# A kernel of three transformer-like layers: VectorE computes the low parts of the weights one chunk of products later

## The reference, cut to what matters

```python
def first_block(...):
    mem_n = rmsnorm(mem, norm_mem)
    for i in range(2):
        h = rmsnorm(x, norm_mix[i])
        mkv = mem_n @ w_mem_kv[i]
        proj = h @ w_in[i]                      # q, k, v, memory q
        y_tok = windowed_gqa(...) if i % 2 == 0 else neighbourhood_attn(...)
        y_mem = memory_attn(...)
        x = x + concatenate([y_tok, y_mem]) @ w_out[i]
        gu = rmsnorm(x, norm_ffn[i]) @ w_gate_up[i]
        x = x + (silu(gu[..., :D_FF]) * gu[..., D_FF:]) @ w_down[i]
    return rmsnorm(x, norm_final)

def second_block(x, c, ...):
    sh1, sc1, ga1, sh2, sc2, ga2 = split(silu(c) @ w_ada + b_ada)
    xn = rms_norm(h, g_mix) * (1 + sc1) + sh1
    q, k, v, qi, ki, wi, xr, yr, gate_a, gate_b = split(xn @ w_in + b_in)   # 5448 wide
    attn = dsa_attention(q, k, v, qi, ki, wi, rel_bias)    # top 64 of 256 by an index score
    rnn = rg_lru(causal_dwconv(xr), ...) * gelu(yr)        # a linear recurrence over time
    merged = sigmoid(gate_a) * (attn @ w_o_attn) + sigmoid(gate_b) * (rnn @ w_o_rnn)
    h = h + ga1 * (merged @ w_out)
    up = causal_dwconv((rms_norm(h, g_ffn) * (1 + sc2) + sh2) @ w_up)
    h = h + ga2 * ((silu(gte) * val) @ w_down)
    return rms_norm(h, g_final)
```

## Time and profile before

| | us |
|---|---|
| median of 3 runs | 1089.95 (1089.11 to 1090.08) |
| the profiled execution | 1088.45 |
| its span in the trace | 1086.5 |
| TensorE busy | 1030.4 (95% of the span) |
| VectorE busy | 734.6 (68%) |
| ScalarE busy | 583.8 (54%) |
| GpSimd busy | 114.9 (11%) |
| mean granted clock of TensorE | 0.982 |
| a piece of w_gate_up, from its issue to its landing | 5.7 |
| TensorE busy between 455 and 605 (second feed-forward) | 150.00 of 150 |
| VectorE busy between 455 and 605 | 121.05 of 150 |
| TensorE busy between 660 and 800 (in-projection of the last layer) | 132.98 of 140 |

### The profile page before, as it was taken

One profiled execution on the slowest core, in us unless ns is written; L12 is line 12 of the kernel. 1 busy time (PEld: TensorE's weight loads), 2 busy tenths in 40 slices (PEclk: granted clock), 3 DMA queues, 4 the chain that ended last, 5 costly groups with the idle time before them and its releaser, 6 DMA issues.

```text
span 1086.5 us, 13575 instructions
## 1 busy us (share of the span) xinstructions
PE 1030.4 (95%) x5216; PEld 855.0 (79%) x5216; DVE 734.6 (68%) x988; ACT 583.8 (54%) x842; POOL 114.9 (11%) x169
## 2 busy tenths in 40 slices
PE   6997999999999989899999999997989999999996
PEld 4876778889888777788888877886878788888885
DVE  4667775666446567578888666779876765777753
ACT  6557564444345557544443354676656456666641
POOL 1013131000000022200000011013630000000001
PEclk9998999999999999999999999998999989999998
DMA  9665379655565431389999896545466435564541
GB/s 335 220 149 81 104 204 285 222 188 177 162 210 188 150 128 41 115 294 351 353 335 327 292 312 217 165 133 156 151 205 213 155 104 189 190 195 156 174 137 39
DMA packets 97984, 211.90 MB, mean 195 GB/s; under 512 B 5681, under 2 KB 13313, under 8 KB 94529
## 3 DMA queue, kind: packets, MB, share of 16 engines
q1 hardware_dynamic: 93313, 194.46, 52.8%
q0 software_dynamic: 4448, 16.51, 6.4%
q10 hardware_dynamic: 160, 0.07, 0.0%
HBM read 206.30 MB, written 6.15 MB: 196 GB/s over the span
## 4 chain that ended last, share of the span: by engine, by line
PE 75%; DVE 10%; ACT 7%; issue 4%; DMA 1%; SPq 1%; POOL 1%; DVEq 0%; ACTq 0%; POOLq 0%
PE bank L878 22%; PE bank L880 22%; PE bank L879 22%; ACT hi L1209 4%; PE bank L856 4%; DVE lo L1641 3%; PE bank L893 1%; PE bank L858 1%; DVE early L1472 1%; DMA raw<-in_w_in 1%; PE bank L1046 1%; DVE xres L1515 1%; DMA small<-in_sink_a 1%; ACT junk L1072 1%; DVE big L1823 0%
## 5 line engine op out<-in xcount | busy, mean ns | idle before, releaser
L1641 DVE TENSOR_TENSOR lo<-raw,hi 128x2048 fp32r<-128x2048 f32 (+1 forms) x164 | 368.6, 2251 | 218.4 <-ACT hi L1209 217.6
L1209 ACT ACTIVATE hi<-raw 128x2048 fp32r<-128x2048 f32 (+1 forms) x164 | 303.3, 1853 | 190.2 <-PE bank L880 148.1
L878 PE MATMUL bank<-hi,xTh 128*128 128x512 f32 (+2 forms) x896 | 345.5, 386 | 3.5 <-DVE lo L1641 3.2
L880 PE MATMUL bank<-hi,xTl 128*128 128x512 f32 (+2 forms) x896 | 337.3, 377 | 0.0
L879 PE MATMUL bank<-lo,xTh 128*128 128x512 f32 (+2 forms) x896 | 336.9, 376 | 0.0
L878 PEld LDWEIGHTS bank<-hi,xTh 128*128 128x128 f32 x896 | 169.9, 190 | 34.3 <-DVE lo L1641 3.8
L880 PEld LDWEIGHTS bank<-hi,xTl 128*128 128x128 f32 x896 | 169.7, 189 | 31.4
L879 PEld LDWEIGHTS bank<-lo,xTh 128*128 128x128 f32 x896 | 170.1, 190 | 28.4
L878 PE MATMUL bank<-hi,hTh 128*128 128x512 f32 x264 | 103.5, 392 | 0.2 <-DVE lo L1641 0.2
L880 PE MATMUL bank<-hi,hTl 128*128 128x512 f32 x264 | 102.8, 389 | 0.0
L879 PE MATMUL bank<-lo,hTh 128*128 128x512 f32 x264 | 102.8, 389 | 0.0
(11 more groups left out here) (355 smaller groups left out, 1328.9 us busy)
## 6 DMA issues: line engine op xcount, KB each, us to landing
raw<-in_w_gate_up SPq DMA_DIRECT2D x44, 1024.0 KB, 5.7
raw<-in_w_down SPq DMA_DIRECT2D x30, 1024.0 KB, 5.1
raw<-in_w_ada SPq DMA_DIRECT2D x24, 1024.0 KB, 6.5
raw<-in_w_up SPq DMA_DIRECT2D x22, 1024.0 KB, 5.2
raw<-in_w_in SPq DMA_DIRECT2D x21, 1024.0 KB, 5.1
raw<-in_w_out SPq DMA_DIRECT2D x12, 1024.0 KB, 5.1
raw<-in_w_in_b SPq DMA_DIRECT2D x10, 1024.0 KB, 5.2
raw<-in_w_in_a SPq DMA_DIRECT2D x6, 1024.0 KB, 9.6
```

The lines of the kernel that those rows point to most:

```text
L878: e.matmul(o, sh, h[:, k, :], start=p.first and k == 0, stop=False)
L880: done = e.matmul(o, sl, h[:, k, :], start=False, stop=p.last and k == p.nk - 1)
L1209: e.activation(hi_s[m % SPLITS][:, 0:n], raw[p.at % RAWS][:, 0:n], ACT.Copy).then_inc(hi_made, 1)
L1641: e.tensor_tensor(lo_s[s][:, 0:n], raw[p.at % RAWS][:, 0:n], hi_s[s][:, 0:n].bitcast(F), ALU.subtract).then_inc(lo_made, 1)
```

## The change

The step "split" of the list now concerns ScalarE alone. For VectorE `split_through` puts a step "low", and "ada" for the modulation weights, into a deque `lows`, and `low_through` writes them to the list. It is called behind each chunk's `between()`, so that of a piece with two chunks the low part stands behind the tasks that follow chunk 0. The start of the kernel and `modulated` call it directly behind `split_through`. The order on TensorE, ScalarE, GpSimd and SyncE stays as it is. Above line 500 the later kernel's line numbers are 10 higher: L1651 is what L1641 was.

```diff
@@ split_through
             if self.plan[i][0] == "ada":
                 self.ada_at[i] = len(self.ada_at) + 1
-                self.steps.append(("ada", i))
+                self.lows.append(("ada", i))
             else:
                 m = self.weights.index(i)
                 self.steps.append(("split", m))
+                self.lows.append(("low", m))
             self.split_next += 1
+
+    def low_through(self):
+
+        while self.lows:
+            self.steps.append(self.lows.popleft())
@@ part
             if ch < p.chunks - 1:
                 between()
+            self.low_through()
         self.owed = m + SPLITS
@@ the program of VectorE
-                if kind == "split":
+                if kind == "low":
```

More of the change, by code:

```diff
@@ L148, in __init__ @@
         self.res_at = {}
+        self.lows = deque()
         self.run()
```

## The result

| | before | after |
|---|---|---|
| median, us | 1090.01 (1089.11 to 1092.04, 4 runs) | 1097.22 (1097.01 to 1098.22, 4 runs) |
| ratio, 95% interval | | 1.0071, 1.0059 to 1.0084 |
| span of the profiled execution, us | 1086.5 | 1095.0 |
| TensorE busy, us | 1030.4 | 1032.9 |
| mean granted clock | 0.982 | 0.981 |

The change makes the kernel slower by 7.2 us; the forecast was 1090.4 with a range up to 1095.5. Slower had 0.32 of the chance, and the time lies above the range.

A forecast was written before the change was run, and what follows sets the result against it. TensorE, busy 1030.4 of 1086.5 us, was taken as the bound, leaving 56.1 us. Gains of -4.4 and losses of +4.85 gave about +0.45 us: 1088.9 profiled, 1090.4 for the median, range 1086.4 to 1095.5.

The forecast's parts named there:

- (b): Second attention: the maximum moves ahead of a low part, removing TensorE's 0.71 us wait for the normalised tile: -0.7 us.
- (c): Top-k attention: two reciprocals come 2.2 us earlier, removing TensorE's 0.93 and 1.81 us waits for GpSimd: -2.7, at least -1.8.
- (a): First attention: VectorE's masking moves ahead of piece 14's low part, two TensorE gaps go: -1.0 us, at least -0.3.
- (d): Memory stage: piece 13's low part comes ahead of an evacuation, delaying a GpSimd chain TensorE waits on: +0.65, or 0.
- (e): First convolution tile: piece 105's low part follows the taps, so a copy TensorE wants ends later: +0.35, between 0 and 0.6.
- (f): Recurrence's gate multiplication: VectorE idles for ScalarE, then the low part delays the copy TensorE's transposes read: +1.2 us.
- (g): Query evacuation after the scan: piece 112's low part comes between, starting it 1.2 us later: +1.2 shared with (f).
- rival A: At the scan GpSimd takes the shared port first, evacuation 3.5 us late: 1095 us; 0.22 with high ends of (g), (h), (i).
- (h): Piece 117's low part goes behind the half-tile task, which waits for GpSimd's scan output: +0.7, middle of 0 to 1.4.
- (i): Merge: piece 127's low part delays the next rTl from 851.17 to 853.1 while TensorE waits: +1.95, between 1.3 and 2.3.
- rival C: Second feed-forward: buffers come free later, so loads come late; four groups at some 1 us each, about 1093.5 us; chance 0.10.
- The bounds: Extremes of the sum, -2.1 to +5.9 us, with TensorE's granted clock named as a further unknown.

The follow-up runs named there:

- only_mem: New order only behind chunk 0 of pieces 0 to 11 (memory stage, first in-projection), against the kernel before: ratio 1.0013 (0.9997 to 1.0029), +1.4 us.
- only_ffn2: New order of low parts and modulation accumulations only in the second feed-forward (pieces 64 to 97), against the kernel before: ratio 1.0026, +2.8 us (1.2 to 4.5).
- gains_again: Second measurement of the kernel with only six low parts moved, behind the attention tasks, against the kernel before: ratio 0.9960, -4.4 us (-6.3 to -2.5).
- only_merge: New order only behind chunk 0 of pieces 124 to 126, the merge, against the kernel before: ratio 1.0032, +3.5 us (1.6 to 5.3).
- not_ffn2: The change everywhere except in the second feed-forward (pieces 64 to 97), against the kernel before: ratio 1.0034, +3.7 us (1.7 to 5.7).
- ffn2_ada3: Only three modulation accumulations in the second feed-forward moved behind a transposed tile, low parts kept in place, against the kernel before: ratio 1.0020, +2.2 us (0.7 to 3.7).

## Why the prediction was wrong

**The gains held.** (b) -0.7: -0.95 by the traces. (c) -2.7: -2.6. (a) -1.0: -1.4 alone, and about +0.2 in the changed kernel, with a half-clock stretch at 112 that the sum didn't have. The three as one kernel: -3.8 and -4.4 for a forecast of -4.4.

**The small losses held.** (d) +0.65: +0.6 by the gap and by only_mem. (e) +0.35: +0.26. (f) +1.2: +1.22. (g): the low part did start first, so rival A didn't come. But (f) and (g) were to share 1.2 us, and TensorE's gap grew from 3.98 to 4.68, so 0.7 us came on top. The scan was to start 1.1 us earlier and starts only 0.3 earlier against the kernel around it, because it now waits for a multiplication of GpSimd. In the trace after, the half-clock stretches that are shorter behind this gap hide the 0.7.

**(h) was mis-sized in the traces.** It was +0.7, "the middle" between 0 and 1.4, and the traces have a gap of 1.75 us where there was none, and piece 117 2.2 us later. The time of the two moves alone, +0.8 (-1.0 to 2.5), can't tell these sizes apart. The mechanism was named, piece 116's low part holding GpSimd up, but I gave it a place in the range and not its price. The price could be worked out from the rows: in the earlier trace rows the low part that comes second takes 1.3 us longer than its 2.25, with 1.4 us left of GpSimd's instruction. Turned round, GpSimd starting 0.15 us behind a low part of 2.25 us has about 2.1 us to wait, and that goes on down a chain with no slack.

**(i) was half of it.** The gap grew by 1.8 us, near the forecast (+1.95). The 1.6 us behind it are the clock. The bounds named such a stretch (+1 to +2.4 for a new gap), but as something beside the sum. No row of before could tell that this gap would bring one, but some of it belonged in the term.

**The step that failed** is that the sum puts the second feed-forward at nothing and leaves late loads to rival C, at 0.10. The prediction said "TensorE runs there without a gap for 150 us, and the low parts catch up within one piece". The margin of the products (2.6 us by the earlier trace rows, measured 1.8) was right, and it was the wrong thing to look at. The low parts did not catch up: piece 74's came 4.5 us late against the kernel around it, and piece 79's still 2.6 us. What is handed on is not a product's margin but a buffer: later low part or accumulation, later load, later high part, and an evacuation behind that low part in VectorE's queue. It was priced at "some 1 us" for each of four groups, +3 in all; the trace shows +4.5 and only_ffn2 +2.8. So its price was fair and its chance wrong. It was also expected in four places, with a product waiting for its high part, and came in two, the larger of them by way of the evacuation. The row against it, TensorE busy for all of 150 us, says nothing of how little slack the buffers have.

**The sum.** The forecast was +0.45. To it come +3.6 (second feed-forward, the mean of 4.5 and 2.8), +1.6 (clock in the merge), +1.5 (h, by the traces) and the first attention's +1.2 with the clock, which makes +8.3 for a measured 7.2 to 7.7. The other shifts of the table that no term had (+0.5, +1.6, -0.5, -2.0 and -0.4) nearly cancel, which is luck: two of them are half-clock stretches that come and go between executions. That all bounds of the sum ended at +5.9 was the same error as the failed step, since C was added to none of them.

## What to carry to other kernels

An instruction that waits for another engine has a use for whatever is queued in front of it: before you move work out from in front of a task, look at what the task waits for, and count the idle time that the moved work was filling. In a stretch where few buffers go round and each waits for a load, a moved step is costed by what it gives free (the buffer, the load behind it, and what is queued behind that load's consumer), not by the margin of its own reader. Move single instructions by the gap that they end, not a whole class: six moves of 67 carried the gain.

## What the runs showed of the hardware

- A gap of 2.26 us on TensorE in the merge was followed by 3.4 us at the 1.2 GHz level in three traces of three, a gap of 0.47 us at the same place in none of fifteen. But equal gaps of 2.4 us near 450 had such a stretch behind them in nine traces (gains_again, only_mem and the changed kernel among them) and not in the nine others (before and only_merge among them). In the second feed-forward gaps of 2.93 and 2.13 us (only_ffn2) and of 2.02 (not_ffn2) had one, and gaps of 2.49 (the changed kernel) and 2.24 (ffn2_ada3) had none. So the length of the gap alone doesn't set it.
- GpSimd's multiplication of 128x1024 took 2.40 us by itself and 4.31 when a low part of 2.26 us with both operands in SBUF had started 0.22 us before; the low part kept its length. So the price of coming second was about the rest of the first one's time, 1.9 us for 2.0.
- Halving 24 of 188 loads brought the DMA share between 455 and 605 from 0.89 to 0.74 and changed the time by -0.1 us (-2.1 to 2.0): the queues were nearly full there, and yet they set no more of the time of the kernel before than those 2 us.
